# Feed-forwards of a two-block transformer kernel: chunks 3 and 4, and 6 and 7, as seven block products of formed sums in place of eight

## The reference

```python
def swiglu_ffn(h, w_gate, w_up, w_down):
    return (jax.nn.silu(h @ w_gate) * (h @ w_up)) @ w_down

h = rms_norm(x, norm_pre[l, 0])
x = x + 0.5 * rms_norm(swiglu_ffn(h, ffn1_w_gate[l], ffn1_w_up[l], ffn1_w_down[l]), norm_post[l, 0])
...
x = x + rms_norm_2(swiglu(h, w_gate[l], w_up[l], w_down[l]), post_ffn_g[l])
```

## Time and profile before

| | us |
|---|---|
| median of 3 runs (2030.54 to 2032.45) | 2030.95 |
| span of the profiled execution | 2030.4 |
| busy TensorE (matmul) | 2010.3 |
| busy VectorE | 1443.8 |
| busy ScalarE | 1120.8 |

### The profile page before, as it was taken

How to read it: one execution, slowest core, us unless ns; L and a number is a source line. 1 busy time by engine, 2 the same in 40 slices (tenths; PEclk the granted TensorE clock), 3 DMA queues, 4 the chain that set the end, 5 groups by cost and what they waited for, 6 DMA issues and landing times.

```text
span 2030.4 us, 24123 instructions
## 1 busy us (share of the span) xinstructions
PE 2010.3 (99%) x9514; PEld 1653.6 (81%) x9514; DVE 1443.8 (71%) x1915; ACT 1120.8 (55%) x1414; POOL 0.2 (0%) x4
## 2 busy tenths in 40 slices
PE   8999999999999999999999999999999999999998
PEld 7888887888888888887888888888888888888887
DVE  6666899776667566999776567966665669667565
ACT  6445667564445455667564446656644457566443
POOL 0000000000000000000000000000000000000000
PEclk9999999999999999999999999999999999999999
DMA  8776764557766775664567767554676675546774
GB/s 262 231 209 176 238 187 145 187 185 214 210 207 222 231 213 176 219 187 147 185 187 222 203 184 222 177 168 139 188 216 205 189 204 186 170 152 187 209 214 122
DMA packets 351410, 394.54 MB, mean 194 GB/s; under 512 B 123825, under 2 KB 259649, under 8 KB 351297
## 3 DMA queue, kind: packets, MB, share of 16 engines
q1 hardware_dynamic: 347200, 381.94, 62.2%
q10 hardware_dynamic: 4096, 11.05, 1.6%
HBM read 365.66 MB, written 1.05 MB: 181 GB/s over the span
## 4 chain that ended last, share of the span: by engine, by line
PE 90%; DVE 5%; ACT 2%; DMA 2%; issue 1%; SPq 0%; ACTq 0%; DVEq 0%
PE ps L622 83%; DVE w_lo L1875 1%; PE ps L693 1%; DVE scratch L2154 1%; PE ps L1204 1%; PE ps L1185 1%; DVE x L1925 0%; ACT w_hi L1264 0%; DMA raw<-in_w_in 0%; DMA raw<-in_w_co 0%; DVE scratch L2191 0%; PE ps L716 0%; DVE scratch L2067 0%; DMA x<-in_x 0%; PE ps L1068 0%
## 5 line engine op out<-in xcount | busy, mean ns | idle before, releaser
L1875 DVE TENSOR_TENSOR w_lo<-raw,w_hi 128x2048 fp32r<-128x2048 f32 x336 | 767.8, 2289 | 217.6 <-ACT w_hi L1264 214.4
L1264 ACT ACTIVATE w_hi<-raw 128x2048 fp32r<-128x2048 f32 (+2 forms) x340 | 644.2, 1897 | 469.0 <-PE ps L622 232.6
L622 PE MATMUL ps<-w_hi,hT_hi 128*128 128x512 f32 x2048 | 806.1, 394 | 0.0
L622 PE MATMUL ps<-w_lo,hT_hi 128*128 128x512 f32 x2048 | 798.2, 390 | 0.0
L622 PE MATMUL ps<-w_hi,hT_lo 128*128 128x512 f32 x2048 | 774.0, 389 | 0.0
L622 PEld LDWEIGHTS ps<-w_hi,hT_hi 128*128 128x128 f32 x2048 | 385.1, 188 | 83.0 <-issue 5.5
L622 PEld LDWEIGHTS ps<-w_hi,hT_lo 128*128 128x128 f32 x2048 | 384.4, 188 | 80.8
L622 PEld LDWEIGHTS ps<-w_lo,hT_hi 128*128 128x128 f32 x2048 | 385.1, 188 | 77.0
L622 PE MATMUL ps<-w_hi,bT_hi 128*128 128x512 f32 x656 | 257.7, 393 | 0.0
L622 PE MATMUL ps<-w_lo,bT_hi 128*128 128x512 f32 x656 | 255.4, 389 | 0.0
L622 PE MATMUL ps<-w_hi,bT_lo 128*128 128x512 f32 x656 | 255.4, 389 | 0.0
(11 more groups left out here) (294 smaller groups left out, 1124.2 us busy)
## 6 DMA issues: line engine op xcount, KB each, us to landing
raw<-in_w_in SPq DMA_DIRECT2D x160, 512.0 KB, 4.6
raw<-in_ffn_w_down SPq DMA_DIRECT2D x88, 512.0 KB, 4.3
raw<-in_ffn_w_gate SPq DMA_DIRECT2D x86, 512.0 KB, 4.0
raw<-in_ffn_w_up SPq DMA_DIRECT2D x86, 512.0 KB, 5.0
raw<-in_w_gate SPq DMA_DIRECT2D x44, 512.0 KB, 4.0
raw<-in_w_up SPq DMA_DIRECT2D x44, 512.0 KB, 5.0
raw<-in_w_down SPq DMA_DIRECT2D x44, 512.0 KB, 4.3
raw<-in_w_out SPq DMA_DIRECT2D x32, 512.0 KB, 4.2
```

Of the source, the lines that this page charges most:

```text
L622: mm = nc.tensor.matmul(bank(t, half), act[:, tiles[i], t * P:(t + 1) * P], w, start=start and (i, n) == steps[0], stop=stop and (i, n) == ...
L1264: nc.scalar.activation(dst, src, ACT.Copy).then_inc(high_ready, 1)
L1875: V.tensor_tensor(lo, src, flat(hi), ALU.subtract).then_inc(low_ready, 1)
```

## The change

In each feed-forward chunks 3 and 4 are made together, and so are 6 and 7 (`PAIRS = (3, 6)`). The activation is seen as four blocks, a11 and a12 (row block 0, first and second 512 of the 1024 columns), a21 and a22 (row block 1). The weights of a pair are four squares of 512 x 512: b11 (gate, first half of the rows), b21 (gate, second half), b12 and b22 (up). The eight block products of the plain form become seven, as in Winograd's form of Strassen's algorithm. Each is a block of 12 matmuls in one PSUM bank and counts as a unit.

- **Sums of activations**, once for each feed-forward: `row_sums` and `row_sums_low` on VectorE, between them a high part on ScalarE (`sum_hi`).
- **Sums of weights**, once for each pair, on VectorE: t1 = b12 - b11, t2 = b22 - t1, t4 = b21 - t2, t3 = b22 - b12 (in place, in the slot of b12). Three of the seven units (products 5, 6 and 4) are such sums and have no load; they get a high and a low part as the others do.
- **Sums of products**, once for each pair, on VectorE: u2, c12, u3, c22, c21, of 128x512 each. ScalarE copies products 1 and 5 out of PSUM first (`hold`).
- A feed-forward has 39 units in place of 33. The slots of `raw` are planned by `_units`; the loads of a pair are four squares and come in the order product 1, product 7, down, product 3, product 2.
- Down of both chunks of a pair follows gate and up of the next chunk (`chunk_behind`).
- Outside the feed-forwards some semaphores are merged under new names, and the zeroing of the convolution's margin moves from the start into the mixer.

The core of the diff, first TensorE:

```diff
+            def pair(c):
+                pe.wait_ge(hid_ready, f * NCHUNK + c)
+                block(c, 1, plain, 0, 0, 4, True)
+                pe.wait_ge(*after("forms", "rows_low", f))
+                block(c, 5, summed, 4, 1, 5, True)
+                down(L, k0 + AT["down", c - 1], c - 1, False)
+                pe.wait_ge(*after("held", f"p1_{c}", f))
+                block(c, 2, plain, 4, 0, 4, False)
+                block(c, 6, summed, 0, 0, 6, True)
+                pe.wait_ge(*after("held", f"p5_{c}", f))
+                block(c, 3, summed, 4, 0, 5, False)
+                pe.wait_ge(*after("forms", f"u2_{c}", f))
+                block(c, 7, summed, 0, 1, 6, False)
+                block(c, 4, plain, 4, 1, 7, True)
```

ScalarE in a pair:

```diff
+                multiplied(L, k0 + AT["down", c - 2])
+                hidden(c - 1)
+                act.wait_ge(*after("forms", f"t2_{c}", f))
+                act.wait_ge(low_ready, pair_unit(L, k0, c, 5) + 1)
+                hold(held_1, 4, 1)
+                form_high(c, 2)
+                hold(held_5, 5, 5)
+                form_high(c, 6)
+                form_high(c, 3)
+                form_high(c, 7)
...
+                form_high(c, 4)
+                for i in (8, 9, 10):
+                    high(L, k + i)
+                act.wait_ge(*after("forms", f"c21_{c}", f))
```

VectorE in a pair, in chunk 2 (`chunk`) and behind a pair:

```diff
+            def pair(k, c):
+                join(c - 1)
+                hidden_low(c - 1)
+                t4(c)
+                weight_low(L, k + 3)
+                weight_low(L, k + 4)
+                t3(c)
+                weight_low(L, k + 5)
+                weight_low(L, k + 6)
+                dve.wait_ge(*after("held", f"p1_{c}", f))
+                pair_sum(c, 6, "u2", sum_2, held_1, ps[:, 6, :])
+                weight_low(L, k + 7)
...
+                pair_sum(c, 3, "c12", sum_2, sum_2, ps[:, 5, :])
...
+                weight_low(L, k + 8)
+                pair_sum(c, 7, "u3", sum_3, held_1, ps[:, 6, :])
...
+                V.tensor_tensor(held_5, sum_3, held_5, ALU.add).then_inc(*done("forms", f"c22_{c}", f))
+                weight_low(L, k + 9)
+                pair_sum(c, 4, "c21", sum_3, sum_3, ps[:, 7, :])
+                weight_low(L, k + 10)
...
+            def chunk(k, c):
+                join(c - 1)
+                if c == 2 and PAIRS:
+                    row_sums_low()
+                if c + 1 in PAIRS:
+                    t1(c + 1)
+                weight_low(L, k + AHEAD)
+                hidden_low(c - 1)
+                weight_low(L, k + 1 + AHEAD)
+                hidden(c)
+                part(c)
+                weight_low(L, k + 2 + AHEAD)
+                if c + 1 in PAIRS:
+                    t2(c + 1)
+
+            def chunk_behind(k, c):
+                join(c - 2)
+                weight_low(L, k + 3)
+                hidden_low(c - 2)
+                join(c - 1)
+                hidden_low(c - 1, second_hi, second_lo)
+                if c + 1 in PAIRS:
+                    t1(c + 1)
+                weight_low(L, k + 4)
+                hidden(c, 4)
+                part(c)
+                weight_low(L, k + 5)
+                weight_low(L, k + 6)
+                if c + 1 in PAIRS:
+                    t2(c + 1)
```

SP in a pair:

```diff
+            def pair(c):
+                square(L, k0 + AT["p", c, 1], wg, 0, c * FC)
+                if c - 3 in PAIRS:
+                    turn_halves(L, n, c - 3)
+                turn_halves(L, n, c - 2)
+                square(L, k0 + AT["p", c, 7], wu, 0, c * FC)
+                down(L, k0 + AT["down", c - 1], wd, c - 1)
+                if c - 3 in PAIRS:
+                    turn_halves(L, n, c - 1)
+                square(L, k0 + AT["p", c, 3], wu, 512, c * FC)
+                if c - 3 not in PAIRS:
+                    turn_halves(L, n, c - 1)
+                square(L, k0 + AT["p", c, 2], wg, 512, c * FC)
```

367 lines of the change are left out of this document (287 added, 80 removed).

## The result

The changed kernel takes 2158.44 us (median; 2157.12 to 2158.57), the kernel before 2031.7 in the same comparison: ratio 1.0623, 95% interval 1.0608 to 1.0638. It is slower by 126.7 us, and the forecast was 2143 with 2105 to 2175 around it. Its profiled execution has a span of 2155.3 us.

The account below looks back on a forecast made before the run. TensorE was taken as the bound, busy 99% of 2030.4 us. Per feed-forward some 23.3 us of waiting less 5.4 saved is 17.9; six times plus 4.8 is 112.2, giving 2143 us, range 2105 to 2175.

Parts of the forecast that it names:

- The bound and the price of a matmul: TensorE, busy 99% of 2030.4 us, bounds the kernel; a matmul costs 0.2267 us, so 144 fewer save 32.6 us.
- Entry: Chunk 2 of each feed-forward: row sums, t1 and hand-over delay hidden 1's low part; down 1 stalls 7.6 us.
- Pair 3 and down 3: VectorE's list runs nearly solid through pair 3: product 3 starts 0.8 us late, down 3 stalls 4.4 us.
- Loads behind transposes: Chunk 5: up-weight loads for pair 6 queue behind SP's transposes, t1 and t2 wait, down 5 stalls 4.8 us.
- Down 6: Pair 6 repeats pair 3: down 6 starts at 581.4 instead of 577.0, a stall of 4.4 us.
- rival (c): TensorE's clock halves after four stalls per feed-forward, 24 x 1.3 = 31 us: 2174; chance 0.10, shared with longer transfers.
- The sum: Six feed-forwards each 17.9 us longer plus 4.8 in the first: 112.2 us on a span of 2030.4, 2142.6.
- the rival's milder form: Only the last stall of each feed-forward pays for the slow clock: 8 us, 2151; counted within the main case's 0.76.
- the small operations: First feed-forward: 22 VectorE operations for rotary tables and casts, between t2 and join 5, add 4.8 us.
- The signs: Profile after: TensorE near 93%, VectorE about 1725 us and a third or more of the chain, waits at down 1, 3, 5, 6.
- Rival (a): Hand-overs cost less, VectorE runs solid, each feed-forward is 2.5 us longer: 2050; chance 0.09 for 2035 to 2100.
- Rival (b): The added VectorE passes hide behind TensorE, giving 1998 to 2015 us; chance 0.04.

Follow-up runs that it names:

- the entry run: Changed kernel with the low part of hidden 1 made directly behind join 1 in chunk 2: 2146.17 us, ratio 1.0562 to the kernel before.
- the filled waits: Changed kernel with ten extra unused 128x512 matmuls ahead of the waits at down 1, 3, 5 and 6: 2147.33 us, ratio 1.0570.
- the last run: Changed kernel with only pair 6, row sums spread over chunks 2 to 4, and low passes, c21 and copies reordered: 2025.60 us, ratio 0.9970.

## Why the prediction was right, point by point

- **The bound and the price of a matmul** held: 144 went, and with the run without pairs showing nothing else, all else is waits, clock and hand-overs.
- **Entry.** Forecast: low part of hidden 1 at 478.7, which is 506.5 on the changed kernel's clock (the first feed-forward had added 27.85), and a wait of 7.6. The low part ended at 504.15 and the wait was 5.34. The term that was mis-sized is the row sums: I priced each of the four short ones at 1.22 us from a row with 1024 columns per partition, but they have 512, and the trace after has 0.69. 4 x 0.53 = 2.1 us. The order that makes the wait was right, as the entry run showed.
- **Pair 3 and down 3**: forecast 553.0 and a wait of 4.4, measured 551.99 and 3.81. Product 3, forecast 0.8 us late, was not. The entry was 2.4 us earlier than forecast and down 3 only 1.0, because t4 waited for its load, as the forecast had it:

```profile
517.14 2.29 DVE L2249 TENSOR_TENSOR scratch<-raw,scratch 128x2048 f32<-128x2048 f32 x1 [2.70 <-DMA raw<-in_ffn_w_gate]
```

- **Loads behind transposes**: forecast that t1 and t2 wait. They waited 1.06 and 3.51, and down 5 came at 573.70 (forecast 574.2). The wait is 3.29 in place of 4.8, because TensorE came 1.1 us later, through the slow clock behind down 3, and the low part 0.5 us earlier.
- **Down 6**: forecast 609.2, measured 609.53, wait 2.54 in place of 4.4: TensorE came 2.1 us later, behind 13 slow matmuls. The three arrivals behind the entry were right within 1.0 us; the waits at the four places were 15.0 in place of 21.2, and slow matmuls and hand-overs filled the difference. A forecast of arrivals held where one of idle time did not. It held beyond the model: in the five feed-forwards behind the first, down 6 comes 140.1 to 142.1 us into its stretch, for a forecast of 140.4.
- **Clock**, rival (c): the mechanism was real. I gave it 1.3 us per wait and said that the first three waits hide it and the last one does not. Behind the last one it cost 1.6 us, and the filled waits gave back 1.9 per feed-forward. The sum had left it out, though the rival's milder form had it (8 us, 2151). The Trainium skill (TensorE: Matmul & The Clock Gate, Part 1) has the half clock as the default that activity lifts. These rows agree: it came back behind waits of 5.3, 3.8, 3.3 and 2.5 us.
- **The sum.** 112.2 us forecast, 124.9 measured between the spans. The first feed-forward has 5.2 of the difference: 27.9 in place of 22.7. Its wait at down 5 is 7.8 in place of 3.3, which is the small operations as forecast; its wait at down 1 is 7.6 in place of 5.3, which I had taken from the second one. The other five have 7.5 together: 2.3, 2.7, -0.4, 1.2 and 1.7. Behind their down 6 stand 7, 6, 0, 6 and 7 matmuls whose next one starts 0.42 to 0.44 us later, 5.2 us in all, and the one feed-forward without them is the one that is not late: the clock behind the last wait is the main missing term. The other 2.3 us I have not placed. The last 2.6 us are in the median, which stands 3.1 us above the span after and stood 0.55 above it before.
- **The signs.** TensorE's share is 95% (forecast 93), VectorE's busy time 1697.7 us (about 1725), its share of the chain 26% (a third or more). One sign of being wrong did come: matmuls behind the waits start 0.43 us apart for 3.9 us behind down 1 and for longer behind down 5, where I had set 3 us. So the list was right and "without the clock" was not; the total stayed near because behind three of four waits the list hides the clock.
- **Rival (a)**, packed, was excluded by VectorE's waits for ScalarE and the transfers, as argued: 2.50 us for the sums' high part, 2.70, 1.06 and 3.51 for loads and twice 3.06 for transposes in the second feed-forward. **Rival (b)**, that the passes hide, needs other places for them, which the last run found for one pair.

## What to carry to other kernels

An algorithm that saves products by adding sums is to be priced by the engine that makes the sums, at the places where that engine's results are asked for, and not by its mean share: here 36% idle did not help, as the first added passes met a join with 5.8 us of slack. Put added passes where that engine waits for something else, and put what the bound engine asks for next at the head of each list; doing so, with one pair dropped, turned 6.2% slower into 0.3% faster. Price a wait of the matmul engine of a few us with the slow matmuls behind it, unless the next thing that it meets is late anyway.

## What the runs showed of the hardware that I had not expected

- Waits of TensorE as short as 2.54 us, and 2.23 in the entry run, were followed by matmuls 0.43 us apart in place of 0.23, 13 of them behind down 5. In the second feed-forward it was 8.0 us, of which only the part with slack behind it counted. The same wait does not always bring it: in the run with one pair down 1 waits 2.93 us both in the second feed-forward, with no slow matmul behind it, and in the sixth, with 7:

```profile
489.61 0.47 PE L737 MATMUL ps<-w_hi,bT_hi 128*128 128x512 f32 x1 [2.93 <-DVE bT_lo L2183]
...
1941.38 0.47 PE L737 MATMUL ps<-w_hi,bT_hi 128*128 128x512 f32 x1 [2.93 <-DVE bT_lo L2183]
...
1943.02 0.63 PE L737 MATMUL ps<-w_hi,bT_hi 128*128 128x512 f32 x1
1943.45 0.63 PE L737 MATMUL ps<-w_lo,bT_hi 128*128 128x512 f32 x1
```

  Behind the waits of 1.0 to 1.9 us of all runs there was none.
- A VectorE pass of 2.3 us beside a GpSimd pass took 6.59, and the GpSimd pass 6.12 in place of 4.6: they don't share, they take turns.
- Matmuls in the pair's blocks (one row block, one PSUM bank) started 0.2308 us apart in place of 0.2266. The cause stays open.
